# A fused block on one core: groups ahead of a norm by pairs of token tiles, and the first feed-forward group by token halves

## The chip, the core and the metric

The kernel runs on one core of one Trainium2 chip. TensorE (PE in the profile) multiplies, VectorE (DVE), ScalarE (ACT) and GpSimd (POOL) work beside it, and SyncE (SP) issues the loads of the weights. The metric is the time in microseconds that the device takes for one execution. Lower is better.

## The reference

Two blocks run on 512 tokens of width 1024, in float32. The first block has two layers (a forget-gate attention and a gated recurrence), the second has one layer (a sparse attention beside a stick-breaking one, then a feed-forward part of width 4096).

```python
for layer in range(DEPTH):                     # first_block
    u = rms_norm(h, norm_pre[layer])
    ...
    h = h + rms_norm(y, norm_post[layer])
    gate = jax.nn.sigmoid((h @ ple_w_gate[layer]).astype(jnp.float32)).astype(h.dtype)
    h = h + (p[layer] @ ple_w_proj[layer]) * gate
...
y = merged @ w_out[l]                          # second_block
x = x + ga1 * rmsnorm(y, g_post_mix[l])
h = rmsnorm(x, g_pre_ffn[l]) * (1.0 + sc2) + sh2
u = jax.nn.relu(h @ w_ff1[l])
y = (u * u) @ w_ff2[l]
x = x + ga2 * rmsnorm(y, g_post_ffn[l])
```

What matters here is that a norm needs a token's whole row. The product ahead of it must be done for all 1024 features before the row can be scaled, and the product behind it needs the scaled row, turned so that features lie on partitions.

## The kernel before, in words

**Numbers.** Each float32 operand is split into a high part and a low part in fp32r, and each product is three matmuls (high with high, high with low, low with high). The helper `three` issues them; its lines are L357 to L359 where tokens are the stationary operand (the result has tokens on partitions) and L353 to L355 where the weights are (features on partitions).

**Weights.** They come in chunks of 128 x 2048 (1 MB) through three slots. SP loads a chunk when its slot is free (semaphore `w_free`), ACT writes its high part (`high`, L755), POOL the low part in four instructions (L331), and then `w_ready` lets PE use it. Each engine's program is a fixed list, so ACT writes a high part only where the list has it.

**Groups.** `group` computes four output tiles of 128 x 512, one PSUM bank each, from two chunks of four K tiles: first all four tiles with chunk 0, then all four with chunk 1. That is 96 matmuls, 48 per chunk; tile m is complete 12 matmuls after tile m-1, and all four complete in the last half of the group. The slot of chunk 0 is given back after 48 matmuls, that of chunk 1 at the end.

**Around the norms.** Three places have this shape. `pg0` and `pg1` are two groups each: their tiles are token tile by 512 features, so tiles 4 to 7 (the second group) hold the second half of the features of token tiles 0 to 3. For each tile ACT takes the sigmoid into `ev` (`gate`, L763), DVE multiplies and adds to the residual `h` (`add_gated`, L1244 and L1245) and ACT squares it for the norm (`square_of_half`, L777). Then DVE makes inverse roots for two token tiles at a time (`roots`, from L1252, 12 small instructions), scales the row (`unit_rows`, L1183 and, from the second norm on, L1185), PE turns the token tile (`turn`, L397, eight transposes), ACT copies the turned tile to `xh` (`turned`, L799) and DVE forms `xl` (`lows`, L1168). PE's next stage `tv1` or `tv2` starts on token tile 0 alone. The third place is `outb2`, one group, with `second_half` (L1206 and L1211) and `whole_rows` (L1191, L1183, L1185) on DVE and `square_of_row` on ACT, then `norm3` (the turns) and `ffn`. There each of the next products runs over all 512 tokens at once, so its first matmul waits for all four token tiles. `ffn` is eight groups of w_ff1 (L353 to L355), each followed one group later by its share of w_ff2.

Of the kernel before, what the change touches and what calls it, by code (L numbers as in the profile page):

```python
# [17 lines left out]
P = 128  # L18
T = 512
TT = T // P  # L20
D = 1024
# [17 lines left out]
ALU = mybir.AluOpType  # L39
# [10 lines left out]
def out_stages(l, extra):  # L50
# [12 lines left out]
    ("outa2", "DDDD", 2, 0, 0), ("outb2", "DDDD", 2, 0, 0), ("norm3", "D" * 8, 0, 0, 0),  # L63
    ("ffn", "AAAA" + "AAAADDDDDDDD" * 7 + "D" * 8, 32, 32, 32),
# [7 lines left out]
SLOTS = 3  # L72
# [26 lines left out]
def build(nc, a):  # L99
    ctx = ExitStack()  # L100
    with ctx:
# [236 lines left out]
        def _(pe):  # L338
# [44 lines left out]

            def groups(name, count, kinds, skip=0, **kw):

                n0, c0 = BASE[name][0] + 4 * skip, BASE[name][1] + 2 * skip
                for g in range(count):
                    group(n0 + 4 * g, c0 + 2 * g, kinds, **kw)
# [151 lines left out]
            def out_and_ple(l):  # L540
# [22 lines left out]
                groups(f"pg{l}", 2, False, tile_ready=lambda m: emptied(n0 + MID_T[m] + 1))  # L563
# [157 lines left out]
            groups("outb2", 1, False)  # L721
            n0 = BASE["norm3"][0]
            for t in range(TT):
                turn(n0 + 2 * t, t, tok["D"], (sg("norm3_xn"), t + 1))
            pe.wait_ge(*emptied(n0 + 7))
            n0, c0, u0, _ = BASE["ffn"]

            n, c = n0, c0
            for i in range(9):
# [13 lines left out]
        def _(act):  # L743
# [96 lines left out]
            def out_and_ple(l):  # L840
# [57 lines left out]
                for m in range(8):  # L898
# [10 lines left out]
                    if m in (4, 5, 6):  # L909
                        square_of_half(m)  # L910
# [202 lines left out]
            for m in range(TT):  # L1113
                square_of_bank("outb2", BASE["outb2"][0] + m, stat[:, 4 + m:5 + m])
                root("outb2", stat[:, 12 + m:13 + m], stat[:, 4 + m:5 + m], stat[:, m:m + 1])
                if m > 0:
                    square_of_row(m - 1)
            turned("norm3", n0, 0)
            square_of_row(3)
            for t in range(1, TT):  # L1120
                turned("norm3", n0 + 2 * t, t)
            high_after("outb2", 1)
            act.wait_ge(sg("post2"), TT)
            act.dma_start(grow[:, :], mods.ap()[5].partition_broadcast(P)).then_inc(sg("grow3"), 16)
            n, c, u, _ = BASE["ffn"]
            for i in range(9):
# [25 lines left out]
        def _(dve):  # L1152
# [71 lines left out]
            def out_and_ple(l):  # L1224
# [41 lines left out]
                unit_rows(name, 0, g, s_)  # L1266
                add_gated(6)
                unit_rows(name, 1, g, s_)
# [339 lines left out]
            second_half(2, 0)  # L1608
            dve.wait_ge(sg("g_row3"), 16)
            dve.wait_ge(sg("s_row3"), 16)  # L1610
            for t in range(TT):
                if t < 3:
                    second_half(2, t + 1)
                if t == 3:
                    lows("norm3", n, 0)
                whole_rows("norm3", t, g_row3, s_row3)
            for t in range(1, TT):
                lows("norm3", n + 2 * t, t)
            n, _, u, s = BASE["ffn"]
            for i in range(9):  # L1620
                if i < 8:
                    for m in range(4):
                        dve.wait_ge(*emptied(n + m))
                        e = ev[:, (u + m) % 4, :]
                        V.after(dve.tensor_tensor(e, e, e, ALU.mult))  # L1625
                        split_tile(e, s + m, Y, 4 * (i % 2) + m).then_inc(ev_free, 1)
# [99 lines left out]
```

## Time and profile before

| | us |
|---|---|
| median of 3 runs | 1809.53 (1806.23 to 1813.26) |
| profiled execution, its time | 1813.34 |
| profiled execution, its span | 1811.5 |
| PE busy | 1662.8 (92% of the span) |
| DVE busy | 857.7 (47%) |
| ACT busy | 602.0 (33%) |
| POOL busy | 591.1 (33%) |
| mean granted TensorE clock | 0.949 of full speed |

The busy time of PE holds matmuls at either clock, so 92% does not say that they ran at full speed. Busy shares are means over a program of some twenty stages; the places where PE stands still are found in the waits and in the timeline.

### The profile page before, as it was taken

What the parts mean: (1) busy time and instruction counts of PE and PEld (TensorE: products, weight loads), DVE (VectorE), ACT (ScalarE), POOL (GpSimd) and SP (SyncE); (2) the same over time, 40 slices, a digit from 0 to 9 for tenths busy, and PEclk for the clock granted to TensorE, in tenths of its full rate; (3) what the DMA queues carried; (4) which work ended last, traced back from release to release, by engine and by line L of the source; (5) the groups of instructions that cost most, each with busy time, mean ns of one, the idle gap of its engine ahead of it and who ended that gap; (6) DMA issues with size and microseconds to landing.
All of it is one profiled execution on the core that took longest, in us unless ns stands there. A gap on an engine that the chain in (4) does not pass through costs nothing.

```text
span 1811.5 us, 20445 instructions
## 1 busy us (share of the span) xinstructions
PE 1662.8 (92%) x7949; PEld 1297.3 (72%) x7949; DVE 857.7 (47%) x1589; ACT 602.0 (33%) x1057; POOL 591.1 (33%) x452
## 2 busy tenths in 40 slices
PE   5899999998998999699899895999999799999998
PEld 4788666776886777577677563666677687777776
DVE  3796465234071777633415588433346532222224
ACT  4321565253222111453332122563433422222222
POOL 3454111343543111234354121221125334444442
PEclk9998999998999999899899587999999799999999
DMA  6775101131233000223222011110123122222221
GB/s 229 279 271 194 47 25 44 63 128 47 96 96 99 24 24 24 70 82 108 87 93 86 9 47 52 47 47 26 45 70 128 58 93 93 93 93 93 93 93 70
DMA packets 86320, 157.05 MB, mean 87 GB/s; under 512 B 3872, under 2 KB 21712, under 8 KB 86224
## 3 DMA queue, kind: packets, MB, share of 16 engines
q1 hardware_dynamic: 81184, 146.81, 24.3%
q10 hardware_dynamic: 5040, 8.94, 1.4%
q8 instruction: 63, 1.03, 0.2%
q14 instruction: 33, 0.27, 0.0%
HBM read 153.62 MB, written 2.12 MB: 86 GB/s over the span
## 4 chain that ended last, share of the span: by engine, by line
PE 80%; DVE 11%; ACT 4%; issue 3%; DMA 2%; POOL 0%; SPq 0%; DVEq 0%; ACTq 0%
PE banks L357 10%; PE banks L358 9%; PE banks L359 9%; PE banks L353 9%; PE banks L354 9%; PE banks L355 8%; PE banks L447 3%; PE banks L449 3%; PE banks L448 3%; PE banks L585 2%; PE banks L697 2%; PE banks L472 2%; PE banks L487 2%; PE banks L497 2%; DVE slot_A L1541 2%
## 5 line engine op out<-in xcount | busy, mean ns | idle before, releaser
L331 POOL TENSOR_TENSOR w_lo<-w_raw,w_hi 128x512 fp32r<-128x512 f32 x448 | 590.9, 1353 | 1191.3 <-ACT w_hi L755 1191.3
L755 ACT ACTIVATE w_hi<-w_raw 128x2048 fp32r<-128x2048 f32 (+1 forms) x114 | 214.4, 1881 | 213.3 <-DMA w_raw<-w_ff_dram 148.5
L353 PE MATMUL banks<-xh,w_hi 128*128 128x512 f32 x672 | 266.9, 397 | 6.5 <-issue 3.9
L354 PE MATMUL banks<-xl,w_hi 128*128 128x512 f32 x672 | 264.4, 393 | 0.0
L355 PE MATMUL banks<-xh,w_lo 128*128 128x512 f32 x672 | 264.1, 393 | 0.0
L357 PE MATMUL banks<-w_hi,xh 128*128 128x512 f32 x384 | 155.6, 405 | 19.3 <-DVE xl L1168 12.9
L357 PE MATMUL banks<-w_hi,yh 128*128 128x512 f32 x384 | 151.6, 395 | 6.6 <-issue 4.2
L353 PEld LDWEIGHTS banks<-xh,w_hi 128*128 128x128 f32 x672 | 128.0, 190 | 41.2 <-issue 10.3
L358 PE MATMUL banks<-w_lo,xh 128*128 128x512 f32 x384 | 153.5, 400 | 0.0
L359 PE MATMUL banks<-w_hi,xl 128*128 128x512 f32 x384 | 153.2, 399 | 0.0
L359 PE MATMUL banks<-w_hi,yl 128*128 128x512 f32 x384 | 149.7, 390 | 0.0
L358 PE MATMUL banks<-w_lo,yh 128*128 128x512 f32 x384 | 149.6, 390 | 0.0
L355 PEld LDWEIGHTS banks<-xh,w_lo 128*128 128x128 f32 x672 | 127.8, 190 | 27.2
L354 PEld LDWEIGHTS banks<-xl,w_hi 128*128 128x128 f32 x672 | 127.9, 190 | 26.6 <-issue 0.5
L763 ACT ACTIVATE ev<-banks 128x512 f32<-128x512 f32 x84 | 50.2, 597 | 262.2 <-PE banks L355 220.1
L447 PE MATMUL banks<-xh,w_hi 128*128 128x512 f32 x256 | 113.9, 445 | 4.7 <-DVE slot_D L1567 2.4
L449 PE MATMUL banks<-xh,w_lo 128*128 128x512 f32 x256 | 102.9, 402 | 0.0
L357 PEld LDWEIGHTS banks<-w_hi,xh 128*128 128x128 f32 x384 | 74.6, 194 | 39.1 <-DVE xl L1168 14.1
L448 PE MATMUL banks<-xl,w_hi 128*128 128x512 f32 x256 | 102.6, 401 | 0.0
L357 PEld LDWEIGHTS banks<-w_hi,yh 128*128 128x128 f32 x384 | 72.1, 188 | 28.7 <-DVE yl L1161 7.3
L359 PEld LDWEIGHTS banks<-w_hi,xl 128*128 128x128 f32 x384 | 74.5, 194 | 16.2
L1625 DVE TENSOR_TENSOR ev<-ev 128x512 f32<-128x512 f32 x32 | 22.2, 693 | 134.7 <-ACT ev L763 134.7
(314 smaller groups left out, 2541.8 us busy)
## 6 DMA issues: line engine op xcount, KB each, us to landing
w_raw<-w_ff_dram SPq DMA_DIRECT2D x32, 1024.0 KB, 5.2
w_raw<-w_in_dram SPq DMA_DIRECT2D x22, 1024.0 KB, 5.0
w_raw<-att_w_in_dram SPq DMA_DIRECT2D x16, 1024.0 KB, 7.5
work_hi<-w_ada_dram SPq DMA_DIRECT2D x16, 1024.0 KB, 7.2
w_raw<-rec_w_in_dram SPq DMA_DIRECT2D x16, 1024.0 KB, 5.4
work_lo<-w_ada_dram SPq DMA_DIRECT2D x8, 1024.0 KB, 6.4
w_raw<-ple_w_gate_dram SPq DMA_DIRECT2D x8, 1024.0 KB, 5.1
w_raw<-att_w_out_dram SPq DMA_DIRECT2D x4, 1024.0 KB, 5.0
```

What stands on the lines that cost most here:

```text
L331: ins = pool.tensor_tensor(wlo[s][:, k, :], raw[s][:, k, :], wh[s][:, k, :].bitcast(F32), ALU.subtract)
L353: pe.matmul(out, w_h, x_h, start=start, stop=False)
L354: pe.matmul(out, w_h, x_l, start=False, stop=False)
L355: return pe.matmul(out, w_l, x_h, start=False, stop=stop)
L357: pe.matmul(out, x_h, w_h, start=start, stop=False)
L358: pe.matmul(out, x_h, w_l, start=False, stop=False)
L359: return pe.matmul(out, x_l, w_h, start=False, stop=stop)
L447: pe.matmul(ps[:, 7, :], w_h, xh[:, k, :], start=k == 0, stop=False)
L448: pe.matmul(ps[:, 7, :], w_h, xl[:, k, :], start=False, stop=False)
L449: mm = pe.matmul(ps[:, 7, :], w_l, xh[:, k, :], start=False, stop=k == 7)
L755: act.activation(wh[s][:, 0:kn, :], raw[s][:, 0:kn, :], ACT.Copy).then_inc(w_split, 1)
L763: act.activation(dst, ps[:, n % 8, :], func, **kw).then_inc(free["A"], 1)
```

## The change

A new helper `group_by_halves` computes a group as tiles 0 and 1 with both chunks, then tiles 2 and 3 with both chunks. It takes the place of `group` for the second group of `pg0` and `pg1` and for `outb2`. The matmuls are the same; chunk 1 is needed after 24 matmuls, where `group` needed it after 48, and the slot of chunk 0 is given back after 72, behind a drain, where it was given back after 48.

The first group of the feed-forward part moves into `norm3` and is divided by token halves: 96 matmuls of 256 columns for tokens 0 to 255, with the turns of token tiles 2 and 3 between its tiles, then 96 for the rest. Both its slots are given back at its end. ACT and DVE are put in the order that fits this.

```diff
-    ("outa2", "DDDD", 2, 0, 0), ("outb2", "DDDD", 2, 0, 0), ("norm3", "D" * 8, 0, 0, 0),
-    ("ffn", "AAAA" + "AAAADDDDDDDD" * 7 + "D" * 8, 32, 32, 32),
+    ("outa2", "DDDD", 2, 0, 0), ("outb2", "DDDD", 2, 0, 0), ("norm3", "D" * 8 + "AAAA", 2, 4, 4),
+    ("ffn", "AAAADDDDDDDD" * 7 + "D" * 8, 30, 28, 28),
...
+            def group_by_halves(n, c, act_h, act_l, tile_ready=None):
+
+                for half in range(2):
+                    for ch in range(2):
+                        if half == 0:
+                            pe.wait_ge(w_ready, c + (ch + 1))
+                        for m in (2 * half, 2 * half + 1):
+                            if ch == 0:
+                                wait_bank(n + m)
+                                if tile_ready:
+                                    pe.wait_ge(*tile_ready(m))
+                            for k in range(4):
+                                mm = three(bank(n + m), (c + ch) % SLOTS, k, act_h, act_l, 4 * ch + k, m, False,
+                                           ch == 0 and k == 0, ch == 1 and k == 3)
+                            if ch == 1:
+                                mm.then_inc(bank_full, 1)
+                        if half == 1:
+                            pe.drain().then_inc(w_free, 1)
...
-                groups(f"pg{l}", 2, False, tile_ready=lambda m: emptied(n0 + MID_T[m] + 1))
+                groups(f"pg{l}", 1, False, tile_ready=lambda m: emptied(n0 + MID_T[m] + 1))
+                group_by_halves(BASE[f"pg{l}"][0] + 4, BASE[f"pg{l}"][1] + 2, xh, xl)
...
-            groups("outb2", 1, False)
-            n0 = BASE["norm3"][0]
-            for t in range(TT):
+            group_by_halves(BASE["outb2"][0], BASE["outb2"][1], xh, xl)
+            n0, c, _, _ = BASE["norm3"]
+            for t in range(2):
                 turn(n0 + 2 * t, t, tok["D"], (sg("norm3_xn"), t + 1))
...
+            for half in range(2):
+                cut = slice(2 * half * P, 2 * half * P + 2 * P)
+                pe.wait_ge(*emptied(n0 + 4 * half + 3))
+                for m in range(4):
+                    for ch in range(2):
+                        s = (c + ch) % SLOTS
+                        if m == 0 and half == 0:
+                            pe.wait_ge(w_ready, c + (ch + 1))
+                        for k in range(4):
+                            out, w = bank(n0 + 8 + m)[:, cut], slice(m * P, m * P + P)
+                            pe.matmul(out, wh[s][:, k, w], xh[:, 4 * ch + k, cut], start=ch == 0 and k == 0, stop=False)
+                            pe.matmul(out, wh[s][:, k, w], xl[:, 4 * ch + k, cut], start=False, stop=False)
+                            mm = pe.matmul(out, wlo[s][:, k, w], xh[:, 4 * ch + k, cut], start=False, stop=ch == 1 and k == 3)
+                    if half == 1:
+                        mm.then_inc(bank_full, 1)
+                    elif m in (1, 2):
+                        turn(n0 + 2 * m + 2, m + 1, tok["D"], (sg("norm3_xn"), m + 2))
+            for ch in range(2):
+                pe.drain().then_inc(w_free, 1)
...
                 add_gated(5)
                 roots(0)
                 unit_rows(name, 0, g, s_)
+                unit_rows(name, 1, g, s_)
                 add_gated(6)
-                unit_rows(name, 1, g, s_)
                 add_gated(7)
```

The order of the instructions shows it at three places. The kernel after has other line numbers: L416 is the turn, L755 to L757 the matmuls of 256 columns, L793 the high part of a chunk, L837 the copy of a turned tile, L815 a square, L826 a root, L801 a gate or a relu.

PE between the turns of the last norm and the first feed-forward group, before (`slot_D` holds the scaled rows, `norm3_xn` says that a row is ready, `free_dve` that DVE has emptied a bank):

```order
L397 MATMUL banks<-ident,slot_D 128x128 [waits free_dve,norm3_xn]
L397 MATMUL banks<-ident,slot_D 128x128 x3
L397 MATMUL banks<-ident,slot_D 128x128 [waits free_dve]
L397 MATMUL banks<-ident,slot_D 128x128 x3
L397 MATMUL banks<-ident,slot_D 128x128 [waits free_dve,norm3_xn]
L397 MATMUL banks<-ident,slot_D 128x128 x3
L397 MATMUL banks<-ident,slot_D 128x128 [waits free_dve]
L397 MATMUL banks<-ident,slot_D 128x128 x3
L353 MATMUL banks<-xh,w_hi 128x512 [waits free_dve,w_ready]
L354 MATMUL banks<-xl,w_hi 128x512
```

After:

```order
L416 MATMUL banks<-ident,slot_D 128x128 [waits free_dve,norm3_xn]
L416 MATMUL banks<-ident,slot_D 128x128 x3
L416 MATMUL banks<-ident,slot_D 128x128 [waits free_dve]
L416 MATMUL banks<-ident,slot_D 128x128 x3
L755 MATMUL banks<-xh,w_hi 128x256 [waits w_ready,free_dve]
L756 MATMUL banks<-xl,w_hi 128x256
L757 MATMUL banks<-xh,w_lo_52 128x256
...
L755 MATMUL banks<-xh,w_hi 128x256 [waits w_ready]
...
L416 MATMUL banks<-ident,slot_D 128x128 [waits free_dve,norm3_xn]
L416 MATMUL banks<-ident,slot_D 128x128 x3
```

The group now begins behind two turns in place of four. It asks for its second chunk (the second `w_ready`) after 12 matmuls, and the other two turns stand between its tiles.

ACT at the same place, before (`slot_C,stat<-h` is `square_of_row`, the L755 with `w_landed2` is the high part of the feed-forward group's second chunk):

```order
L799 ACTIVATE xh<-banks 128x4x128 [waits bank_full] x2
L777 ACTIVATE slot_C,stat<-h 128x1024 [waits outb2_squared,post2]
L788 ACTIVATE stat<-stat,small_columns 128x1 [waits norm3_squared]
L799 ACTIVATE xh<-banks 128x4x128 [waits bank_full] x6
L755 ACTIVATE w_hi<-w_raw 128x2048 [waits w_landed2]
L1124 DMA gain_row<-mod_rows 128x1024 [waits post2]
L755 ACTIVATE w_hi<-w_raw 128x2048 [waits w_landed0]
L763 ACTIVATE ev<-banks 128x512 [waits bank_full,ev_free] x4
L755 ACTIVATE w_hi<-w_raw 128x2048 [waits w_landed1]
```

After:

```order
L837 ACTIVATE xh<-banks 128x4x128 [waits bank_full] x4
L815 ACTIVATE slot_C,stat<-h 128x1024 [waits outb2_squared,post2]
L826 ACTIVATE stat<-stat,small_columns 128x1 [waits norm3_squared]
L815 ACTIVATE slot_C,stat<-h 128x1024 [waits outb2_squared,post2]
L826 ACTIVATE stat<-stat,small_columns 128x1 [waits norm3_squared]
L793 ACTIVATE w_hi<-w_raw 128x2048 [waits w_landed2]
L837 ACTIVATE xh<-banks 128x4x128 [waits bank_full] x4
L1168 DMA gain_row<-mod_rows 128x1024 [waits post2]
L793 ACTIVATE w_hi<-w_raw 128x2048 [waits w_landed0]
L801 ACTIVATE ev<-banks 128x512 [waits bank_full,ev_free] x4
L793 ACTIVATE w_hi<-w_raw 128x2048 [waits w_landed1]
```

The turned tiles 0 and 1 come first, then two squares of rows, then the same high part, then tiles 2 and 3. The last row of each list (`w_landed1`) is the high part of the second chunk of the next feed-forward group; it stands behind the four relus in both.

ACT in the second group of `pg0`, before, from the second gate of that group on:

```order
L763 ACTIVATE ev<-banks 128x512 [waits bank_full,ev_free]
L777 ACTIVATE slot_C,stat<-h 128x512 [waits tv1_squared,pg0_h]
L763 ACTIVATE ev<-banks 128x512 [waits bank_full,ev_free]
L777 ACTIVATE slot_C,stat<-h 128x512 [waits tv1_squared,pg0_h]
L755 ACTIVATE w_hi<-w_raw 128x2048 [waits w_landed0]
L763 ACTIVATE ev<-banks 128x512 [waits bank_full,ev_free]
```

After (the first row holds the first two gates):

```order
L801 ACTIVATE ev<-banks 128x512 [waits bank_full,ev_free] x2
L815 ACTIVATE slot_C,stat<-h 128x512 [waits tv1_squared,pg0_h] x2
L801 ACTIVATE ev<-banks 128x512 [waits bank_full,ev_free]
L815 ACTIVATE slot_C,stat<-h 128x512 [waits tv1_squared,pg0_h]
L793 ACTIVATE w_hi<-w_raw 128x2048 [waits w_landed0]
L801 ACTIVATE ev<-banks 128x512 [waits bank_full,ev_free]
```

The first two squares stand together behind the second gate. The last gate keeps its place behind the high part of a chunk (`w_landed0`).

## Rows read from the trace of the kernel before

**Rows 1.** The page, part 4: shares of the chain that ended last, by engine.
```profile
PE 80%; DVE 11%; ACT 4%; issue 3%; DMA 2%; POOL 0%; SPq 0%; DVEq 0%; ACTq 0%
```

**Rows 2.** PE's waits over the span: total us, times, longest us.
```profile
PE banks L397 <- DVEq L1186: 33.1, 9, 13.8
...
PE banks L357 <- DVE xl L1168: 12.9, 3, 5.6
```

**Rows 3.** Windows: us, busy (count) per engine, granted TensorE clock, DMA share, GB/s.
```profile
403.10:424.80 21.70, 21.70 (x96) 17.91 (x96) 6.38 (x17) 8.40 (x14) 10.02 (x8) 1.00 0.30 97
424.80:436.00 11.20, 3.42 (x19) 2.44 (x17) 8.69 (x12) 5.39 (x10) 5.08 (x4) 0.67 0.29 95
858.20:870.40 12.20, 3.17 (x18) 2.44 (x17) 10.94 (x12) 5.39 (x10) 5.10 (x4) 0.66 0.27 88
1421.10:1439.70 18.60, 7.13 (x33) 5.56 (x32) 17.48 (x24) 9.37 (x18) 0.00 (x0) 0.61 0.22 70
1439.70:1445.70 6.00, 6.00 (x14) 4.75 (x15) 0.00 (x0) 2.44 (x2) 5.28 (x5) 0.50 0.14 51
997.60:1001.90 4.30, 4.27 (x39) 4.30 (x39) 4.12 (x3) 0.00 (x0) 4.08 (x3) 1.00 0.00 0
```

**Rows 4.** Timeline of PE around the last norm: start us, us, instruction, [idle before].
```profile
1399.19 0.47 PE L357 MATMUL banks<-w_hi,xh 128*128 128x512 f32 x1 [0.26 <-issue]
...
1421.70 1.09 PE L397 MATMUL banks<-ident,slot_D 128*128 128x128 f32 x8 [0.46 <-DVEq L1186]
...
1464.79 0.47 PE L353 MATMUL banks<-xh,w_hi 128*128 128x512 f32 x1 [0.26 <-issue]
```

**Rows 5.** Timeline of POOL: the low parts of weight chunks, four instructions each.
```profile
406.03 10.02 POOL L331 TENSOR_TENSOR w_lo<-w_raw,w_hi 128x512 fp32r<-128x512 f32 x8 [14.63 <-ACT w_hi L755]
...
430.92 5.84 POOL L331 TENSOR_TENSOR w_lo<-w_raw,w_hi 128x512 fp32r<-128x512 f32 x4 [14.87 <-ACT w_hi L755]
...
1401.87 10.04 POOL L331 TENSOR_TENSOR w_lo<-w_raw,w_hi 128x512 fp32r<-128x512 f32 x8 [9.39 <-ACT w_hi L755]
```

**Rows 6.** Timeline of ACT in pg0: gates L763, squares L777, chunk split L755.
```profile
417.09 0.60 ACT L763 ACTIVATE ev<-banks 128x512 f32<-128x512 f32 x1 [6.75 <-PE banks L359]
...
419.43 0.63 ACT L777 ACTIVATE slot_C<-h 128x512 f32<-128x512 f32 x1 [1.74 <-DVEq L1247]
...
428.32 0.63 ACT L777 ACTIVATE slot_C<-h 128x512 f32<-128x512 f32 x1 [4.82 <-DVEq L1247]
...
428.95 1.90 ACT L755 ACTIVATE w_hi<-w_raw 128x2048 fp32r<-128x2048 f32 x1
...
430.75 0.58 ACT L763 ACTIVATE ev<-banks 128x512 f32<-128x512 f32 x1
```

**Rows 7.** Timeline of ACT before and in the last norm.
```profile
1404.44 1.92 ACT L755 ACTIVATE w_hi<-w_raw 128x2048 fp32r<-128x2048 f32 x1 [2.65 <-DMA w_raw<-w_ff_dram]
...
1424.05 1.06 ACT L777 ACTIVATE slot_C<-h 128x1024 f32<-128x1024 f32 x1 [1.75 <-DVE h L1211]
...
1425.43 1.06 ACT L799 ACTIVATE xh<-banks 128x512 fp32r<-128x512 f32 x2
```

**Rows 8.** Timeline of DVE: low part in tv1, then the last norm.
```profile
434.65 1.29 DVE L1168 TENSOR_TENSOR xl<-banks,xh 128x512 fp32r<-128x512 f32 x2 [0.25 <-DVE h L1245]
...
1421.73 0.69 DVE L1206 TENSOR_TENSOR slot_B<-banks,gain_row 128x512 f32<-128x512 f32 x1
...
1424.12 1.28 DVE L1183 SCALAR_TENSOR_TENSOR slot_D<-h,stat,slot_A 128x1024 f32<-128x1024 f32 x1
...
1426.81 0.69 DVE L1206 TENSOR_TENSOR slot_B<-banks,gain_row 128x512 f32<-128x512 f32 x1
...
1431.88 1.29 DVE L1168 TENSOR_TENSOR xl<-banks,xh 128x512 fp32r<-128x512 f32 x2
```

**Rows 9.** Timeline of DVE in pg1: inverse roots begin; the row of tile 0 has ended.
```profile
856.16 0.16 DVE L1252 TENSOR_TENSOR stat<-stat 128x2 f32<-128x2 f32 x1 [0.94 <-ACT slot_C L777]
...
861.09 0.69 DVE L1244 TENSOR_TENSOR ev<-ev,slot_A 128x512 f32<-128x512 f32 x1
```

More of the change, by code:

```diff
@@ L720, in _ @@
             groups("outa2", 1, False, ready=(sg("merged"), 0))
-            groups("outb2", 1, False)
-            n0 = BASE["norm3"][0]
-            for t in range(TT):
+            group_by_halves(BASE["outb2"][0], BASE["outb2"][1], xh, xl)
+            n0, c, _, _ = BASE["norm3"]
+            for t in range(2):
                 turn(n0 + 2 * t, t, tok["D"], (sg("norm3_xn"), t + 1))
[L725 to L729, printed above, removed]
+            for half in range(2):
[17 more added lines that the diff above has]
+                pe.drain().then_inc(w_free, 1)
+            n, c, _, _ = BASE["ffn"]
+            u0 = BASE["norm3"][2]
+            for i in range(1, 9):
                 if i < 8:
@@ L908, in out_and_ple @@
                         square_of_half(3)
-                    if m in (4, 5, 6):
+                    if m in (5, 6):
+                        if m == 5:
+                            square_of_half(4)
                         square_of_half(m)
@@ L1112, in _ @@
             act.wait_ge(sg("outa2_eps"), 1)
[L1113 to L1117, printed above, removed]
+            for half in range(2):
+                for m in (2 * half, 2 * half + 1):
+                    square_of_bank("outb2", BASE["outb2"][0] + m, stat[:, 4 + m:5 + m])
+                    root("outb2", stat[:, 12 + m:13 + m], stat[:, 4 + m:5 + m], stat[:, m:m + 1])
+                if half == 0:
+                    square_of_row(0)
+                    square_of_row(1)
             turned("norm3", n0, 0)
+            turned("norm3", n0 + 2, 1)
+            square_of_row(2)
             square_of_row(3)
-            for t in range(1, TT):
-                turned("norm3", n0 + 2 * t, t)
             high_after("outb2", 1)
+            turned("norm3", n0 + 4, 2)
+            turned("norm3", n0 + 6, 3)
             act.wait_ge(sg("post2"), TT)
             act.dma_start(grow[:, :], mods.ap()[5].partition_broadcast(P)).then_inc(sg("grow3"), 16)
+            n, c, u, _ = BASE["norm3"]
+            high(c + 2)
+            for m in range(4):
+                empty_to_ev(n + 8 + m, u + m, ACT.Relu)
+            high(c + 3)
             n, c, u, _ = BASE["ffn"]
-            for i in range(9):
+            for i in range(1, 9):
                 if i < 8:
@@ L1608, in _, with squared_relu @@
             second_half(2, 0)
+            second_half(2, 1)
             dve.wait_ge(sg("g_row3"), 16)
             dve.wait_ge(sg("s_row3"), 16)
[L1611 to L1618, printed above, removed]
+            whole_rows("norm3", 0, g_row3, s_row3)
+            whole_rows("norm3", 1, g_row3, s_row3)
+            second_half(2, 2)
+            second_half(2, 3)
+            lows("norm3", n, 0)
+            lows("norm3", n + 2, 1)
+            whole_rows("norm3", 2, g_row3, s_row3)
+            whole_rows("norm3", 3, g_row3, s_row3)
+            lows("norm3", n + 4, 2)
+            lows("norm3", n + 6, 3)
+            def squared_relu(n, u, s, i):
+                for m in range(4):
+                    dve.wait_ge(*emptied(n + m))
+                    e = ev[:, (u + m) % 4, :]
+                    V.after(dve.tensor_tensor(e, e, e, ALU.mult))
+                    split_tile(e, s + m, Y, 4 * (i % 2) + m).then_inc(ev_free, 1)
+            squared_relu(n + 8, BASE["norm3"][2], BASE["norm3"][3], 0)
             n, _, u, s = BASE["ffn"]
-            for i in range(9):
+            for i in range(1, 9):
                 if i < 8:
[L1622 to L1626, printed above, removed]
+                    squared_relu(n, u, s, i)
                     n, u, s = n + 4, u + 4, s + 4
```

## The prediction

> **What bounds the kernel now.** I read the chain that ended last first: 80% of the span is PE and 11% DVE [rows 1]. So PE sets the end, and only places where PE stands still, or runs at half clock, can give time back. The waits of PE come next: 33.1 us for scaled rows ahead of a turn and 12.9 us for `xl` [rows 2]. Some of that lies in the start and in other norms. The windows show the three places that the change touches [rows 3]. From the end of `pg0` at 424.8 to the first matmul of `tv1` at 436.0 there are 11.2 us, of which the two turns are the only PE work. From the end of `pg1` to `tv2` there are 12.2 us. From the end of `outb2` at 1421.1 to the first feed-forward matmul at 1439.7 there are 18.6 us. Behind the last one PE runs at 1.2 GHz for 6.0 us (granted clock 0.50, 14 matmuls, 0.43 us each), where a full clock gives 96 matmuls in 21.7 us, 0.227 each [rows 3]. The timelines [rows 4 to 9] say who keeps PE there, and in the kernel after, who will.
>
> All sums are made against the profiled span of 1811.5 us, whose own time is 1813.34. It is 0.1% above the median of 1809.53, so I carry differences over unchanged.
>
> **pg0 and tv1.** The second group starts at 403.1. Its first 24 matmuls end at 408.6 (24 x 0.227 = 5.45). Now chunk 1 is wanted there. POOL works on two chunks in one row from 406.03 for 10.02 us, so the first is done at 411.0 [rows 5]; before, PE came to it at 414.0 and never waited. So PE stands 2.5 us, and all tiles of the group move: tile 0 is full at 413.8, tile 1 at 416.5, the slot of chunk 0 is free at about 422.3 with the added drain (0.3), tile 2 is full at 425.1, tile 3 at 427.8.
>
> The norm chain of tiles 0 and 1 starts 3 us earlier and is no longer late. What is late next is the last gate, which is queued on ACT behind a chunk split: gate to square 2.34 us, square to split 0.63, split to last gate 1.80, last gate to `xl` 3.90 [rows 6, 8]. From tile 2 full at 425.1, with 0.2 us for its end to be seen, that puts the last gate at 425.3 + 2.34 + 0.63 + 1.80 = 430.1 in place of 430.75. The chunk itself is no later: its slot is free at 422.3, and from a free slot to the split is 5.5 us in this trace (outa2 ends 0.26 us before 1399.19, the split of the chunk that took its slot starts at 1404.44) [rows 4, 7], so 427.8. PE starts `tv1` **0.7 us** earlier.
>
> **pg1 and tv2** repeat this with a shift added to each row. The group ends at 858.2 [rows 3] and so starts at 836.3; POOL is late there by the same 2.5 us. Tile 1 is full at 849.7; gate and additions 2.34, its square 0.7 give 852.9; roots and the first row take 4.93 [rows 9]; the second row, now put ahead of the third addition, 2.69 [rows 8], so 860.5; addition 1.5, and the square starts near 862.1, 0.6 us before its old time. I take **0.5 us**.
>
> **outb2, the last norm and the first feed-forward group.** The group starts at 1399.2 and wants its second chunk at 1404.7. POOL begins two chunks at 1401.87 and takes 10.04 us, so the first is ready at 1406.9 [rows 5]. PE stands 2.3 us. Tile 0 is full at 1409.7, tile 1 at 1412.4, the slot of chunk 0 free at 1418.2, tile 2 full at 1421.0, tile 3 at 1423.7.
>
> DVE takes some 2.4 us for a `second_half` and 2.7 for a `whole_rows` (from 1421.73 to 1424.12 and on to 1426.81) [rows 8]. Both pairs for tiles 0 and 1 end at about 1421.4, the `second_half` of tile 3 at 1426.9. The turns of tiles 0 and 1 follow the group at once. ACT copies them by 1427 (1.06 each) [rows 7], the two `xl` are done at 1429.4 (1.29 each) [rows 8], and PE starts the group at about **1429.4, 10.3 us earlier** than before.
>
> Most of it is then given back, in this order. (a) After 12 matmuls of 256 columns, at 1430.8, PE wants the second chunk. It landed long ago, but ACT does its high part behind the two copies and two squares of rows, 1.38 us each [rows 7]: 1427.1 + 2.8 = 1429.9. With 1.9 for the high part [rows 6] and 5.84 for POOL while DVE is busy [rows 5] it is ready at 1437.6; with 5.02 (half of 10.04) at 1436.8. PE stands **6.3 us**; behind it in PE's queue are 84 matmuls and two turns. (b) The two turns that lay in the gap now lie between matmuls, 0.9 us each at full clock (1.09 with the last one's tail) [rows 4]: **1.8**. (c) The halves cost 192 instructions where 96 were. The trace has no fp32r matmul of 256 columns. One of 512 takes 0.227, half of which is 0.114. Loads bound it from below: matmuls of 72 columns, each with a new 128 x 128 weight, come every 4.30/39 = 0.110 us [rows 3]. I take 0.115, as the 72-column row has the same load and the stream is no longer than half of 0.227: 22.1 us against 21.8, **0.3**. The upper bound is load and stream one after the other, 0.110 + 0.114 = 0.224. (d) The half clock behind the stall stays, since PE is as idle before 1437 as before 1439.7: 6.0 us at half speed, 3.0 lost, as before. The second half of tokens waits for nothing: the last turn ends near 1448, its `xl` follows in 3.
>
> Sum: 1437.2 + 84 x 0.115 + 1.8 + 2.9 (clock) = 1451.6, plus 96 x 0.115 = 1462.6, plus 0.6 for the drains, 1463.2; before, the next group began at 1464.79 [rows 4]. Then (e): both slots come free only now, so the next group's second chunk has its high part at 1463.2 + 5.5 = 1468.7 to 1470.6 and its low part at 1475.6, where PE wants it at 1463.2 + 10.9 = 1474.1: **1.5 us** of standing. Of 1.6 us gained 0.1 is left. SP and POOL keep their order, and no transfer is added.
>
> **Loads.** The Trainium skill ("TensorE: Matmul & The Clock Gate", Part 3) says that a weight load overlaps matmuls in flight only when it targets other rows of the array. By that rule the halved matmuls would pay their 96 added loads in full. The same page (Part 2) says that a load is pulled ahead of running matmuls into a background buffer, which would hide them. By the first the sum becomes 1829, the slower rival below; by the second it stays 1808. The trace speaks for the second at 512 columns: 96 matmuls with 96 loads take 0.227 us each at full clock and 0.43 at half clock [rows 3], nearly twice, with no room for a load of 0.110 in the smaller.
>
> **Sum.** 0.7 + 0.5 + 0.1 = 1.3 us off 1811.5. On the median: **1808 us**.
>
> **Rivals.** *Nothing waits for the chunks* (faster): if POOL and ACT run so that (a), (e) and the 2.3 us in `outb2` cost nothing, the gain is 1.3 + 6.3 + 1.5 + 2.3 = 11.4, so 1798. For it: the chunk of (a) lies in its slot at 1424. Against: ACT's list has the split behind the squares. It becomes faster by over 0.5% from 9 us, so needs nearly all of it. Chance 0.11. *Short stalls drop the clock* (same, at the upper edge): five new stalls of 1.5 to 6.3 us. In [rows 3] the clock fell within gaps of 11 to 19 us; if it also fell behind the three of 2.5 us, at 3.0 each, the time is 1808 + 9 = 1817. Chance 0.12. *Halved matmuls don't hide their loads* (slower): at 0.224 us each, 192 x 0.109 = 21 us more, so 1829; it decides from 10.3 us above my sum, which is 0.169 us per matmul. Against: the 72-column row. Chance 0.06. *The split brings nothing*: if DVE gets to the `xl` of tiles 0 and 1 no earlier than before, at 1439.7 (it has one queue, with the last tile's `second_half` ahead of them), the stall of (a) vanishes, but (b), (c) and (e) stay: 1.8 + 0.3 + 1.5 less the 1.2 of the two gates, 1811. A slip up to 1436 costs nothing, as (a) hides it. Chance 0.08. My forecast itself: 0.63.
>
> **Range.** The likeliest case alone is 1804 to 1813 (clock phase 3 us up or down, matmul at 0.110 to 0.125, runs that spread by 3.5 us). With the rivals up to 1 in 10 on each side: 1800 to 1817. About 0.5% (9 us) is what a measurement of this kernel can tell from no change. Faster by more: 0.12; slower by more: 0.09; same: 0.79.
>
> **What would show it.** Right: PE idle for 2 to 3 us after the first 24 matmuls of `outb2` and of the second groups of `pg0` and `pg1`, released by POOL; the first 256-column matmul about 6 us after the end of `outb2` in place of 18.6; a wait for POOL of about 6 us behind its twelfth, and one of 1 to 2 us in the group after; 256-column matmuls every 0.11 to 0.12 us. Wrong: 256-column matmuls at 0.17 or more, no wait for POOL behind the twelfth, or granted clock 0.5 inside `pg0`, `pg1` or `outb2`.

## The result, and the profile after

The changed kernel takes 1814.69 us (median of 11 runs, 1811.77 to 1817.43), the kernel before 1811.38 in the runs beside it (11 runs, 1806.23 to 1814.18). The ratio is 1.0024, with a 95% interval of 1.0015 to 1.0034: about 4.4 us slower, 3.3 by the medians. I had forecast 1.3 us faster. The time lies within the range, which was 17 us wide, and within what I called "same", but its sign is the wrong one, and the interval excludes the forecast.

The page after, part 4, shares of the chain that ended last (before: [rows 1]):

```profile
PE 78%; DVE 9%; ACT 4%; issue 3%; DMA 2%; POOL 2%; PEld 1%; SPq 0%; DVEq 0%; ACTq 0%; PEldq 0%
```

PE and DVE have lost two points each, POOL has won two and PEld, the weight loads, one. PE's waits say where POOL comes in (total us, times, longest us; before: [rows 2]):

```profile
PE banks L357 <- DVE xl L1217: 17.2, 3, 6.5
PE banks L416 <- DVEq L1235: 14.2, 1, 14.2
PE banks L357 <- POOL w_lo L331: 11.2, 4, 4.7
...
PE banks L755 <- POOL w_lo L331: 6.8, 1, 6.8
...
PE banks L755 <- DVE xl L1217: 3.3, 1, 3.3
...
PE banks L353 <- POOL w_lo L331: 1.1, 1, 1.1
```

The wait for scaled rows fell from 33.1 us to 14.2, and the one that is left lies outside the change. In its place stand longer waits for `xl` (17.2 us at L357, where it was 12.9, and 3.3 at L755) and waits for POOL's low parts of weight chunks (L331); of the four at L357 the one of 4.7 us lies outside the change. The timeline of PE gives their places (start us, us, instruction, [idle before]; before: [rows 4]):

```profile
401.75 0.47 PE L357 MATMUL banks<-w_hi,xh 128*128 128x512 f32 x1 [0.26 <-issue]
409.72 0.50 PE L357 MATMUL banks<-w_hi,xh 128*128 128x512 f32 x1 [2.25 <-POOL w_lo L331]
...
434.01 0.80 PE L357 MATMUL banks<-w_hi,xh 128*128 128x512 f32 x1 [5.09 <-DVE xl L1217]
...
833.78 0.47 PE L357 MATMUL banks<-w_hi,xh 128*128 128x512 f32 x1 [0.26 <-issue]
841.75 0.50 PE L357 MATMUL banks<-w_hi,xh 128*128 128x512 f32 x1 [2.25 <-POOL w_lo L331]
...
869.10 0.80 PE L357 MATMUL banks<-w_hi,xh 128*128 128x512 f32 x1 [6.54 <-DVE xl L1217]
...
1396.98 0.47 PE L357 MATMUL banks<-w_hi,xh 128*128 128x512 f32 x1 [0.26 <-issue]
1404.72 0.50 PE L357 MATMUL banks<-w_hi,xh 128*128 128x512 f32 x1 [2.02 <-POOL w_lo L331]
...
1428.82 0.38 PE L755 MATMUL banks<-xh,w_hi 128*128 128x256 f32 x1 [3.29 <-DVE xl L1217]
1438.21 0.58 PE L755 MATMUL banks<-xh,w_hi 128*128 128x256 f32 x1 [6.81 <-POOL w_lo L331]
1464.21 0.47 PE L353 MATMUL banks<-xh,w_hi 128*128 128x512 f32 x1 [0.37 <-issue]
1476.43 0.50 PE L353 MATMUL banks<-xh,w_hi 128*128 128x512 f32 x1 [1.07 <-POOL w_lo L331]
...
1510.71 0.47 PE L353 MATMUL banks<-xh,w_hi 128*128 128x512 f32 x1 [0.26 <-issue]
```

All five waits of the forecast are there, near their sizes. Windows behind the three short ones show what I had put at nothing (columns as in [rows 3]):

```profile
409.72:415.20 5.48, 5.48 (x24) 4.55 (x25) 1.63 (x1) 0.60 (x1) 4.93 (x4) 1.00 0.00 0
841.75:845.70 3.95, 3.95 (x10) 3.16 (x11) 0.00 (x0) 0.00 (x0) 3.95 (x4) 0.57 0.00 0
845.70:850.00 4.30, 4.30 (x20) 3.54 (x19) 1.56 (x3) 1.41 (x3) 0.94 (x1) 1.00 0.00 0
1404.72:1408.90 4.18, 4.18 (x11) 3.32 (x12) 0.00 (x0) 0.00 (x0) 4.18 (x4) 0.59 0.00 0
```

In `pg0` 24 matmuls follow in 5.48 us at full clock. In `pg1` and `outb2` ten and eleven take four us. In narrow windows the granted clock is 0.50, which is 1.2 GHz, from 842.2 to 845.6 and from 1405.4 to 1408.8, and 1.00, 2.4 GHz, just ahead and just behind. So the clock fell within 0.7 us of the first matmul behind the wait, for 3.4 us each time.

The two profiled spans (1811.5 and 1812.3) differ by only 0.8 us. Outside the changed places the profile after is 2.8 us shorter. Of this, 1.35 lie ahead of `pg0`'s second group, where nothing was changed. About 1 lies right behind the first matmuls of `tv1` and `tv2`: TensorE is at half clock there for 5.4 and 3.8 us, where it was for 6.1 and 5.2 before. The forecast had no term for it, and the stretches leave it out. I compare by stretches between marks, here and for the runs below: from the second group's start to the first matmul of `tv1`, the same to `tv2`, and from the start of `outb2` to the second w_ff1 group behind the divided one (1510.71 here; 1509.94 in the kernel before).

| kernel | pg0 to tv1 | pg1 to tv2 | outb2 on | sum against before | medians apart |
|---|---|---|---|---|---|
| before | 32.89 | 34.12 | 110.75 | | |
| after | 32.26 | 35.32 | 113.73 | +3.6 | +3.3 |
| 1 pairs ahead of tv only | 32.28 | 35.30 | 110.52 | +0.3 | +0.5 |
| 2 last norm only | 32.86 | 34.13 | 114.00 | +3.2 | +4.0 |
| 3 halves only | 32.88 | 34.14 | 116.34 | +5.6 | +7.5 |
| 4 four chunks early | 29.79 | 32.28 | 106.12 | -9.6 | -8.0 |
| 5 three chunks early | 29.76 | 32.28 | 109.76 | -6.0 | -7.5 |
| 6 the fourth early | 33.78 | 33.73 | 110.73 | +0.5 | +0.2 |
| 7 halves by chunk, all early | 29.77 | 32.25 | 101.34 | -14.4 | -14.2 |
| 8 before, halves by chunk | 32.87 | 34.13 | 112.08 | +1.3 | +1.5 |
| 9 as 7, gate first | 29.35 | 30.42 | 98.70 | -19.3 | -20.6 |
| 10 short rows | 32.30 | 35.34 | 110.96 | +0.8 | +0.5 |

The stretches are those of one execution each, the medians those of 4 to 12. The sums follow the medians within 2 us, so little else changed.

### The profile page after: what moved, and what is told of

Same layout as the page of the kernel before. It is cut to its first block, busy times and chain, and to the rows that moved or that the text cites. A ratio compares the mean times of both kernels' runs of the same rounds, so it can differ in the third digit from the quotient of the medians.

```text
span 1812.3 us, 20635 instructions
## 1 busy us (share of the span) xinstructions
PE 1660.2 (92%) x8045; PEld 1298.5 (72%) x8045; DVE 862.2 (48%) x1589; ACT 602.1 (33%) x1057; POOL 593.7 (33%) x452
## 4 chain that ended last, share of the span: by engine, by line
PE 78%; DVE 9%; ACT 4%; issue 3%; DMA 2%; POOL 2%; PEld 1%; SPq 0%; DVEq 0%; ACTq 0%; PEldq 0%
PE banks L357 10%; PE banks L359 9%; PE banks L358 9%; PE banks L353 8%; PE banks L355 8%; PE banks L354 8%; PE banks L466 3%; PE banks L468 3%; PE banks L467 3%; PE banks L605 2%; PE banks L717 2%; PE banks L491 2%; POOL w_lo L331 2%; PE banks L506 2%; PE banks L516 2%
## 5 line engine op out<-in xcount | busy, mean ns | idle before, releaser
L331 POOL TENSOR_TENSOR w_lo<-w_raw,w_hi 128x512 fp32r<-128x512 f32 x448 | 593.5, 1358 | 1188.7 <-ACT w_hi L793 1188.7
L793 ACT ACTIVATE w_hi<-w_raw 128x2048 fp32r<-128x2048 f32 (+1 forms) x114 | 214.5, 1881 | 221.8 <-DMA w_raw<-w_ff_dram 154.6
L353 PE MATMUL banks<-xh,w_hi 128*128 128x512 f32 x640 | 253.3, 396 | 5.8 <-issue 4.0
L354 PE MATMUL banks<-xl,w_hi 128*128 128x512 f32 x640 | 250.8, 392 | 0.0
L355 PE MATMUL banks<-xh,w_lo 128*128 128x512 f32 x640 | 250.7, 392 | 0.0
L357 PE MATMUL banks<-w_hi,xh 128*128 128x512 f32 x384 | 157.1, 409 | 30.5 <-DVE xl L1217 17.2
L357 PE MATMUL banks<-w_hi,yh 128*128 128x512 f32 x384 | 151.5, 394 | 6.6 <-issue 4.2
L353 PEld LDWEIGHTS banks<-xh,w_hi 128*128 128x128 f32 x640 | 121.2, 189 | 38.8 <-issue 10.2
L354 PEld LDWEIGHTS banks<-xl,w_hi 128*128 128x128 f32 x640 | 121.3, 189 | 25.4 <-issue 0.5
L355 PEld LDWEIGHTS banks<-xh,w_lo 128*128 128x128 f32 x640 | 121.1, 189 | 25.6
L801 ACT ACTIVATE ev<-banks 128x512 f32<-128x512 f32 x84 | 50.3, 598 | 257.6 <-PE banks L355 189.5
L466 PE MATMUL banks<-xh,w_hi 128*128 128x512 f32 x256 | 113.5, 443 | 4.7 <-DVE slot_D L1616 2.4
L357 PEld LDWEIGHTS banks<-w_hi,xh 128*128 128x128 f32 x384 | 75.1, 196 | 52.5 <-DVE xl L1217 18.0
L468 PE MATMUL banks<-xh,w_lo 128*128 128x512 f32 x256 | 102.0, 398 | 0.0
L467 PE MATMUL banks<-xl,w_hi 128*128 128x512 f32 x256 | 101.6, 397 | 0.0
L357 PEld LDWEIGHTS banks<-w_hi,yh 128*128 128x128 f32 x384 | 72.1, 188 | 28.7 <-DVE yl L1210 7.4
L358 PEld LDWEIGHTS banks<-w_lo,xh 128*128 128x128 f32 x384 | 75.1, 196 | 15.3
```

The costliest lines, as they stand in the source:

```text
L331: ins = pool.tensor_tensor(wlo[s][:, k, :], raw[s][:, k, :], wh[s][:, k, :].bitcast(F32), ALU.subtract)
L353: pe.matmul(out, w_h, x_h, start=start, stop=False)
L354: pe.matmul(out, w_h, x_l, start=False, stop=False)
L355: return pe.matmul(out, w_l, x_h, start=False, stop=stop)
L357: pe.matmul(out, x_h, w_h, start=start, stop=False)
L358: pe.matmul(out, x_h, w_l, start=False, stop=False)
```

## The experiments

Theory 1: waits for POOL's low part, and the clock that falls behind them, eat the gain at all three places. Theory 2: the loss is in the feed-forward part alone.

**1. The pairs ahead of tv1 and tv2 alone.** `outb2`, `norm3` and the feed-forward part as before. Against the kernel before, with ACT and DVE in the order that fits it:

```diff
-                groups(f"pg{l}", 2, False, tile_ready=lambda m: emptied(n0 + MID_T[m] + 1))
+                groups(f"pg{l}", 1, False, tile_ready=lambda m: emptied(n0 + MID_T[m] + 1))
+                group_by_halves(BASE[f"pg{l}"][0] + 4, BASE[f"pg{l}"][1] + 2, xh, xl)
```

> The part of the change in pg0 and pg1 alone. In the profile of the whole change this part gave 0.7 us at tv1 and lost 1.2 us at tv2, where the clock fell to half for 3.4 us behind the wait of 2.25 us for POOL. Theory 1 (a short wait in the middle of a group costs more than itself, since the clock may fall behind it): between -1.4 and +3 us against before, about +0.5, and at least one of the two waits in the profile with a granted clock of 0.5 behind it. Theory 2 (the loss is all in the feed-forward part): -1.2 us.

Measured: 1811.71, ratio 1.0004 (0.9994 to 1.0013). `tv1` came 0.6 us earlier, `tv2` 1.2 us later, with the clock at half from 842.3 to 845.7. So this part gains nothing by itself, as theory 1 has it; the 1.2 us less of theory 2 are at the very edge of the interval.

**2. The last norm and the feed-forward part alone.** Against the kernel after, `pg0` and `pg1` put back:

```diff
-                groups(f"pg{l}", 1, False, tile_ready=lambda m: emptied(n0 + MID_T[m] + 1))
-                group_by_halves(BASE[f"pg{l}"][0] + 4, BASE[f"pg{l}"][1] + 2, xh, xl)
+                groups(f"pg{l}", 2, False, tile_ready=lambda m: emptied(n0 + MID_T[m] + 1))
```

> The part of the change in outb2, the last norm and the first feed-forward group alone; pg0 and pg1 as before. From the profile of the whole change it loses 1.7 us up to the next group and 1.1 us in a wait for POOL there. Theory 1: +2.8 us against before, or +1.1 if the clock does not fall behind the wait in outb2. Theory 2: the whole measured loss and the gain of the other part, +5 to +6 us.

Measured: 1815.23, ratio 1.0022 (1.0013 to 1.0031). Most of the loss is here. The median lies between the two theories' numbers and decides nothing between them. What the two parts give together (0.5 and 4.0) is the whole change (3.3 by the medians, 4.4 by the ratio) within the noise.

**3. The halves alone.** All four token tiles are turned first, as before; then the first w_ff1 group runs by token halves, in the order of the change.

```diff
+                    for half in range(2):
+                        cut = slice(2 * half * P, 2 * half * P + 2 * P)
+                        for m in range(4):
...
+                            for ch in range(2):
...
+                    for ch in range(2):
+                        pe.drain().then_inc(w_free, 1)
```

> The kernel before, with only the first feed-forward group computed by token halves behind all four turns (192 matmuls of 256 columns, both slots given back at its end). Matmuls of 0.119 us as in the profile of the whole change: 192 x 0.119 - 96 x 0.227 = +1.1 us, and a wait for POOL in the next group of 1.1 us: +2.2 us. If the halves are free (0.114 us each) and only the wait counts: +1.1 us. If loads were not hidden (0.22 us each): +20 us.

Measured: 1818.65, ratio 1.0043 (1.0026 to 1.0059), far more than expected. Its timeline of PE says why:

```profile
1439.99 0.58 PE L742 MATMUL banks<-xh,w_hi 128*128 128x256 f32 x1 [1.80 <-DVE xl L1189]
1445.71 0.58 PE L742 MATMUL banks<-xh,w_hi 128*128 128x256 f32 x1 [2.80 <-POOL w_lo L331]
1469.48 0.47 PE L353 MATMUL banks<-xh,w_hi 128*128 128x512 f32 x1 [0.37 <-issue]
1481.52 0.50 PE L353 MATMUL banks<-xh,w_hi 128*128 128x512 f32 x1 [0.90 <-POOL w_lo L331]
```

The chunk is wanted after 12 matmuls and isn't ready in the kernel before either: PE waits 2.8 us, and 0.9 in the next group. I had counted only the second of these (1.1). Against the kernel before, the stretches give 5.6 us and the medians 7.5; what makes the other 2 us of the medians is open.

**4. Four high parts earlier.** ACT writes the high part of the second chunk of both `pg` groups, of `outb2` and of the divided group ahead of the gates or squares that it stood behind.

```diff
+                    if m == 2:
+                        high_after(f"pg{l}", 1)
                     gate(m)
...
-                        high_after(f"pg{l}", 1)
...
+                if m == 2:
+                    high_after("outa2", 1)
...
-            high_after("outa2", 1)
...
+            high_after("outb2", 1)
             turned("norm3", n0 + 2, 1)
             square_of_row(2)
             square_of_row(3)
-            high_after("outb2", 1)
```

> The whole change, with four high parts moved ahead in ACT's list: in pg0 and pg1 that of the second group's second chunk ahead of the third gate, in outa2 that of outb2's second chunk ahead of the third square, in the last norm that of the feed-forward group's second chunk ahead of the last two squares of rows. Theory 1: the three waits of 2.0 to 2.3 us and the half clock behind two of them vanish (6.5 + 3.4 us), and the wait of 6.8 us behind the twelfth halved matmul falls to about 3 or 4: 12 to 13 us less than the whole change, so -8 to -9 us against before. Theory 2: the three short waits are hidden by other work, only the last shrinks: 3 us less than the whole change, within 1 us of before.

Measured: 1803.23, ratio 0.9955 (0.9940 to 0.9970): 8.0 us under the kernel before, as expected, and 11.5 under the changed kernel. No short wait is left, and the clock stays up inside the three groups. 3.42 us of the long wait stay.

**5 and 6. That edit divided.** 5 has the lines for `pg` and `outa2` alone, for the three short waits:

```diff
+                    if m == 2:
+                        high_after(f"pg{l}", 1)
...
+                if m == 2:
+                    high_after("outa2", 1)
```

6 has the line for `outb2` alone, for the long wait:

```diff
+            high_after("outb2", 1)
             turned("norm3", n0 + 2, 1)
```

> This is the changed kernel with one edit: ACT writes the high part of the second weight chunk of outb2 and of the second groups of pg0 and pg1 one or two instructions earlier (ahead of the squares and gates that it was queued behind), so that POOL can follow in time. The feed-forward chunk is left as it is. The run before it that moved all four chunks gained 11.5 us on the changed kernel (1803.2 against 1814.7); this one and the next divide that gain. Theory 1 (a wait of 2.0 to 2.3 us for a chunk costs itself, and 1.7 us more where TensorE's clock falls to 1.2 GHz for 3.4 us behind it): the three waits and both falls of the clock are gone, pg0 to tv1 gets 2.5 us shorter, pg1 to tv2 3.0, outb2 to the first feed-forward matmul 3.9, the wait of 6.8 us behind the twelfth halved matmul stays: 1805 to 1807. Theory 2 (the whole loss and the whole gain lie in the feed-forward part): 1813 to 1815.

Measured: 1804.09, ratio 0.9964 (0.9951 to 0.9978), 0.9 us under the range of theory 1 and far from that of theory 2. Its three groups take 22.69 us each from their first matmul to the first turn (425.32 - 402.63, 851.63 - 828.94, 1411.80 - 1389.11), where after's take 25.23, 26.84 and 26.61. In `pg0` that is the wait of 2.25 us and 0.3 us that starting again costs beside it; in `pg1` and `outb2`, where the clock had fallen, it is 1.6 us more. `pg1` gives 1.1 of it back, in a longer wait for `xl`: DVE bounds the end there.

> The changed kernel with the other edit alone: ACT writes the high part of the second feed-forward chunk ahead of the squares of the last two rows instead of behind them. The three short waits stay. Theory 1: the wait behind the twelfth halved matmul shrinks from 6.8 to about 3.4 us, and nothing else moves: 1811. Theory 2: the gain of 11.5 us is here, 1803 to 1804.

Measured: 1811.83, ratio 0.9999 (0.9990 to 1.0008). The long wait shrank from 6.81 to 4.39 us, less than forecast. So most of the gain of experiment 4 came from the three short waits. What the fourth chunk adds to them is 3.6 us by the stretches, but 0.5 by the medians apart and 1.6 by the ratios, which five runs can't size; alone, on the changed kernel, it brings 3.1 both by the stretches and by the medians apart. Windows behind its three short waits:

```profile
410.02:413.30 3.28, 3.28 (x8) 2.63 (x9) 0.00 (x0) 0.00 (x0) 3.28 (x3) 0.50 0.00 0
841.53:845.50 3.97, 3.97 (x17) 3.29 (x18) 0.10 (x1) 0.60 (x1) 3.97 (x4) 1.00 0.00 0
1401.71:1406.50 4.79, 4.79 (x14) 3.77 (x15) 0.00 (x0) 0.37 (x1) 4.79 (x4) 0.65 0.00 0
```

Now the clock fell in `pg0` and stayed up in `pg1`, the reverse of after, with the same instructions up to there and the same waits. The two runs price a fall: `pg0` to `tv1` 33.78 with, 32.26 without; `pg1` to `tv2` 35.32 with, 33.73 without: **1.5 to 1.6 us**.

**7. The divided group by chunk.** As 4, and within a token half all four tiles take chunk 0, then all four chunk 1:

```diff
-                for m in range(4):
-                    for ch in range(2):
-                        s = (c + ch) % SLOTS
-                        if m == 0 and half == 0:
-                            pe.wait_ge(w_ready, c + (ch + 1))
+                for ch in range(2):
+                    s = (c + ch) % SLOTS
+                    if half == 0:
+                        pe.wait_ge(w_ready, c + (ch + 1))
+                    for m in range(4):
...
+                        if half == 0 and (ch, m) in ((0, 3), (1, 1)):
+                            turn(n0 + 4 + 2 * ch, 2 + ch, tok["D"], (sg("norm3_xn"), 3 + ch))
```

> All four chunks early, and in addition the divided feed-forward group runs inside each token half first over all four tiles with chunk 0, then over all four with chunk 1, with the turn of token tile 2 behind the first 48 matmuls and that of tile 3 behind 24 more. So the second chunk is wanted after 48 matmuls and not after 12, and the slot of chunk 0 comes free after three quarters of the group and not at its end. Against the run with the four early chunks (1803.2): by theory 1 the wait of 3.4 us goes (of which some 1 us comes back, since 48 matmuls and not 12 now run at half clock, and a wait for the last turned tile may come), and the wait of 1.1 us in the next group goes: 1799 to 1801. If the order of the matmuls costs something of its own (other banks in turn, more waits), 1803 or more.

Measured: 1797.43, ratio 0.9922 (0.9909 to 0.9934), better than expected. PE waits for POOL neither in the group nor in the next:

```profile
1422.95 0.58 PE L755 MATMUL banks<-xh,w_hi 128*128 128x256 f32 x1 [3.29 <-DVE xl L1219]
1451.24 0.47 PE L353 MATMUL banks<-xh,w_hi 128*128 128x512 f32 x1 [0.26 <-issue]
1473.52 0.47 PE L357 MATMUL banks<-w_hi,yh 128*128 128x512 f32 x1 [0.26 <-issue]
```

**8. The same order in the kernel before**: the matmuls of 3 in the order of 7, all turns first. Against experiment 3:

```diff
-                        for m in range(4):
-                            for ch in range(2):
+                        for ch in range(2):
+                            for m in range(4):
...
-                    for ch in range(2):
-                        pe.drain().then_inc(w_free, 1)
+                            if half == 1:
+                                pe.drain().then_inc(w_free, 1)
```

> The kernel before with only the first feed-forward group divided by token halves, as in the run that took 1818.7, but in each half all four tiles with chunk 0 and then all four with chunk 1. All token tiles are turned before it starts, as before. Theory 1: the 7.5 us that run lost were a wait of 2.8 us and one of 0.9 us for chunks, and 1.3 us for matmuls of 256 columns every 0.119 us and two drains, with the rest in the spread of the kernel before; so with both waits gone the loss is 1.3 us to 2 us: 1812.5 to 1813. Rival: the halved matmuls themselves cost it (loads that are not hidden, another clock): 1816 to 1818.

Measured: 1813.12, ratio 1.0006 (0.9997 to 1.0014). The halved matmuls and the drain cost 1.3 us by the stretches. The other 4.3 us of experiment 3's stretches are its two waits (3.7) and twice the 0.3 us for starting again.

**9. The last gate.** As 7, and at the end of `pg0` and `pg1` ACT splits the last chunk right behind the gate of tile 6 and gates tile 7 next. Against experiment 7:

```diff
-                    if m == 7:
-                        high_after(f"pg{l}", 3)
...
                     gate(m)
+                    if m == 6:
+                        high_after(f"pg{l}", 3)
```

(The square of tile 6 moves behind the gate of tile 7.)

> The best version so far (1797.4) with one edit at the ends of pg0 and pg1: ACT writes the high part of the last weight chunk directly behind the gate of tile 6, when ACT has nothing else, and takes the gate of tile 7 directly behind it, ahead of the square of tile 6. In the run before, that gate stood behind the square and the high part: in pg1 tile 7 was full at about 856, its gate began at 860.4, and DVE was idle for 3.2 us until then with the first xl of tv2 behind it. Theory (the prediction's: behind the pairs, the last gate is late because of the split it is queued behind, and it alone keeps tv1 and tv2 back): the first matmul of tv1 comes about 2 us earlier and that of tv2 about 4 us earlier, 1790.5 to 1792. Rival (the additions on DVE, which POOL's low part now overlaps, or the squares and roots behind them, take the place of the gate): less than half of it, 1794.5 to 1797.

Measured: 1790.45, ratio 0.9888 (0.9872 to 0.9905): the best version, 20.6 us under the kernel before. But the expectation was hit for the wrong reason. In `pg1` the gate came 3.5 us earlier, and `tv2` only 1.8; `tv1` gained 0.4. The other 2.6 us by the stretches are in the feed-forward part, which the edit doesn't touch: in this execution the clock was at full speed from the first 256-column matmul, in that of experiment 7 at half until 1429.1. Why it did not fall here is open, and of the 7.0 us between the medians only these 2.3 can be given to the edit. DVE at the end of `pg1`:

```profile
855.60 0.69 DVE L1296 TENSOR_TENSOR ev<-ev,slot_A 128x512 f32<-128x512 f32 x1
856.32 1.77 DVE L1297 TENSOR_TENSOR h<-h,ev 128x512 f32<-128x512 f32 x1
858.33 1.43 DVE L1296 TENSOR_TENSOR ev<-ev,slot_A 128x512 f32<-128x512 f32 x1 [0.24 <-DVE h L1297]
859.80 1.63 DVE L1297 TENSOR_TENSOR h<-h,ev 128x512 f32<-128x512 f32 x1
861.68 1.29 DVE L1220 TENSOR_TENSOR xl<-banks,xh 128x512 fp32r<-128x512 f32 x2 [0.25 <-DVE h L1297]
```

An addition takes 0.69 us alone and 1.4 to 1.8 beside POOL's low part, which the early split has brought there. The last gate ended at 856.7, but DVE came to its addition only at 858.33, since the rows and the additions of the tile before it were in the way. So by what moved in `pg0` and `pg1` (2.3 us of 6) the rival of this run holds; only the time did not show it.

**10. Short rows.** The changed kernel, with DVE's two instructions for the rows of token tiles 2 and 3 cut to 64 columns.

```diff
+                w = 64 if name == "norm3" and t > 1 else 1024
-                xn = tok["D"][:, t, :]
+                xn = tok["D"][:, t, 0:w]
```

> The changed kernel, with the rows of token tiles 2 and 3 of the last norm scaled and shifted in their first 64 of 1024 columns only (the rest of these rows is left as it was, so the feed-forward input of tokens 256 to 511 is not the reference's). It takes away most of DVE's work while POOL forms the low part that the twelfth halved matmul waits for (7.22 us there, 5.04 where DVE is idle); nothing else that this wait depends on changes. If DVE's work beside it slows POOL: the four instructions take 5.0 to 5.4 us, the wait shrinks from 6.8 to about 4.8 us, 1812.5 to 1813. Rival (ACT's copies, PE's reading or the place itself slow it): still 7 us or more, 1814.7.

Measured: 1811.53, ratio 1.0002 (0.9992 to 1.0011). POOL's low part of the chunk after, then in this run, and what DVE does in the changed kernel meanwhile:

```profile
1430.94 7.22 POOL L331 TENSOR_TENSOR w_lo<-w_raw,w_hi 128x512 fp32r<-128x512 f32 x4 [21.32 <-ACT w_hi L793]
...
1431.76 1.86 DVE L1232 SCALAR_TENSOR_TENSOR slot_D<-h,stat,slot_A 128x1024 f32<-128x1024 f32 x1
1433.65 2.17 DVE L1234 TENSOR_TENSOR slot_D<-slot_D,slot_A 128x1024 f32<-128x1024 f32 x1
```

```profile
1430.60 4.92 POOL L331 TENSOR_TENSOR w_lo<-w_raw,w_hi 128x512 fp32r<-128x512 f32 x4 [21.35 <-ACT w_hi L793]
```

Without DVE's rows the same four instructions take 4.92 us, and PE's wait is 4.56 us in place of 6.81 (expected about 4.8; the time is 1 us under its range). POOL and DVE hold each other up: DVE's two rows above take 4.03 us, and 2.50 where POOL is idle. The Trainium skill ("SBUF — State Buffer", section "SBUF: two separate sides") says that a DVE instruction with two SBUF inputs and a GpSimd one that reads SBUF exclude each other for a whole instruction. The sizes agree: POOL lost 2.3 us, and the two DVE instructions take 1.28 and 1.22 us where POOL is idle, 2.5 together.

## Why the prediction was wrong

By the stretches the change cost 3.6 us, where I had 1.3 gained: 4.9 us off. Three terms make it up.

**The clock behind the short waits** (3.0 us: 1.7 in `pg1`, 1.3 behind `outb2`). I priced the waits behind the 24th matmul and left the clock at full, with 0.12 for a rival in which it falls. That step failed, and it is the largest term: each fall cost 1.6 us. (Behind `outb2` 0.3 of it is made up for, as the wait itself was 2.02 us and not 2.3.) In the runs that have such a wait of 2.0 to 2.3 us (after, 1, 2, 6, 10) the clock fell behind 8 of 12: all four in `outb2`, three of four in `pg1`, one of four in `pg0`. Behind the seven waits of 0.8 to 1.1 us in the next group (after, 2 to 6, 10) it never fell, and neither did it in any of the twelve groups of experiments 4, 5, 7 and 9, which have no wait. Two falls were in the profile after; my rival had three at 3.0. What tips it at one place and not at another is open. In `outb2` the fall made everything behind it late: the high part of the next chunk began at 1428.96, 32.0 us behind the group's start, where the forecast had 30.7.

**POOL's low part** (1.8 us). This term was mis-sized. I took 5.0 to 5.8 us for it from [rows 5], and it took 7.22. The row of 5.84 had two DVE additions of 128 x 512 beside it, the new place has rows of 128 x 1024; experiment 10 shows that DVE makes the difference. The wait itself was only 0.5 longer than forecast (6.81, forecast 6.3), since PE came late to it too: 1.6 us by the fall in `outb2`, and 1.2 because the clock fell at 1429.2, so that the first twelve halved matmuls took 2.6 us, where the forecast had them at full clock and 1.4.

**Small ones, 0.1 together.** The 256-column matmuls come every 0.119 to 0.12 us at full clock (0.213 at half), not 0.115:

```profile
1449.41 0.28 PE L756 MATMUL banks<-xl,w_hi 128*128 128x256 f32 x1
1449.53 0.28 PE L757 MATMUL banks<-xh,w_lo 128*128 128x256 f32 x1
1449.65 0.28 PE L755 MATMUL banks<-xh,w_hi 128*128 128x256 f32 x1
```

That is 192 x 0.004 = 0.8 us more. Half clock behind the stall was shorter (4.7 us, until 1442.9, forecast 6.0), and from the end of the long wait to the next group there were 26.0 us, as forecast (1463.2 - 1437.2).

**What was right.** `tv1` came 0.6 us earlier (forecast 0.7). `tv2`, where the clock did not fall (experiment 6), 0.4 (forecast 0.5). The three waits were 2.25, 2.25 and 2.02 (2.5, 2.5, 2.3), the last gate was what is late next, the group in `norm3` began 31.8 us behind `outb2`'s start (30.2; the fall is the difference), and the next group lost 1.4 (1.5).

**The rivals.** *Nothing waits for the chunks*: false as the change was made, but this is what the experiments built; 4 and 7 gained 8 and 14 us. *Halved matmuls don't hide their loads*: false. By the Trainium skill's rule on other rows of the array ("TensorE: Matmul & The Clock Gate", Part 3) a 256-column matmul would come every 0.224 us by the sum of [rows 3]; 0.12 was measured, with a new 128 x 128 weight each. *The split brings nothing*: false; the first feed-forward matmul did come 8.7 us earlier against the start of `outb2` (forecast 10.3). It was given back in the queue behind it, as forecast. (The terms of that rival add up to 1812, not 1811.)

## What to carry to other kernels

Dividing a group so that its first tiles are complete sooner also calls its second weight chunk sooner. Look at who prepares that chunk, and move the preparation with the division: here the change alone lost 3 to 4 us; with ACT's list in step (no new work, other positions) it gained 8, and with the order of chunks 14. With the last gate it was 21, of which the profiles show 2.3 for the gate itself.

A short stall of TensorE is not priced by its length alone. One of 2.0 to 2.3 us cost itself and 0.3, and in 8 of 12 cases 1.6 us more for the clock; one of about 1 us (1.07) cost 1.4 in all.

Before an instruction is moved to an idle spot, see whether that puts POOL beside two-input instructions of DVE: both get slower, and what was to gain by it may wait for either.

## What the runs showed of the hardware

- The clock fell behind 8 of 12 waits of 2.0 to 2.3 us, for 3.4 us each time (1.5 to 1.6 us lost), and behind none of seven waits of 0.8 to 1.1 us. In `pg0` and `pg1` it fell at different ones of the two in two executions whose instructions are the same up to there.
- A low part of four POOL instructions takes 4.92 to 5.05 us with DVE idle and 7.22 beside rows of 1024; those rows then take 1.86 and 2.17 us in place of 1.28 and 1.22. DVE's `xl`, which has one operand in PSUM, is not held up: two take 1.29 us beside POOL (at 434.65 in the kernel before, [rows 8] and [rows 5]) and 1.29 with POOL idle (at 1442.85 in experiment 10).
- fp32r matmuls of 256 columns with a fresh weight each come every 0.12 us, against 0.227 for 512 columns.
